# Two expert mixtures: blocks of 32 tokens on four 32-column lanes in place of blocks of 64 on two lanes

## What is computed

```python
g_sel = argmax(h @ grp_w + grp_b)                 # one of 4 groups
e_p, e_i = top_k(softmax(logits of the group's 8 experts), 2)
for each token and each of its two experts e:
    hid = silu(x @ w_gate[e]) * (x @ w_up[e])     # 1024 -> 512
    out[token] += weight * (hid @ w_down[e])      # 512 -> 1024
```

## Time and profile before

| | |
|---|---|
| median of 3 runs | 2241.99 us (2241.41 to 2243.58) |
| the profiled execution | 2241.24 us |
| its span | 2239.5 us |
| PE, weight loads, DVE, ACT busy | 95%, 62%, 49%, 27% of the span |
| read from DRAM | 614.42 MB, 281 GB/s over the span |
| of it expert weights | 64 experts of 3 slabs |
| mean granted TensorE clock | 0.991 of full speed |
| mixture 0 | from 311.6 us to 839 us |
| mixture 1 | from 1000.4 us to 1464 us |

### The profile page before, as it was taken

How to read it: one execution, slowest core, us unless ns; L and a number is a source line. 1 busy time by engine, 2 the same in 40 slices (tenths; PEclk the granted TensorE clock), 3 DMA queues, 4 the chain that set the end, 5 groups by cost and what they waited for, 6 DMA issues and landing times.

```text
span 2239.5 us, 31551 instructions
## 1 busy us (share of the span) xinstructions
PE 2134.6 (95%) x12424; PEld 1387.6 (62%) x12424; DVE 1086.9 (49%) x1971; ACT 595.2 (27%) x1200; POOL 12.7 (1%) x20
## 2 busy tenths in 40 slices
PE   7999999999898989899999999999999999999998
PEld 4744654444343437574444444478989988998997
DVE  5677541111111126642222222167888777787876
ACT  4446632211111114531111111033441012434001
POOL 0000000000000010000000000000000000000000
PEclk9999999999999999999999999999999999999999
DMA  8289268998999995248999999962345546235452
GB/s 351 76 353 427 85 254 360 380 383 346 429 381 430 428 402 221 113 157 343 427 428 428 428 429 428 426 252 107 121 170 188 188 160 254 105 118 203 185 189 97
DMA packets 50144, 629.95 MB, mean 281 GB/s; under 512 B 5888, under 2 KB 6912, under 8 KB 11904
## 3 DMA queue, kind: packets, MB, share of 16 engines
q1 hardware_dynamic: 45008, 611.30, 67.1%
q10 hardware_dynamic: 2880, 9.44, 1.0%
q0 software_dynamic: 2160, 7.87, 0.9%
HBM read 614.42 MB, written 14.16 MB: 281 GB/s over the span
## 4 chain that ended last, share of the span: by engine, by line
PE 70%; DMA 16%; DVE 9%; ACT 2%; issue 1%; SPq 0%; POOL 0%; ACTq 0%; POOLq 0%; DVEq 0%
PE ps L1954 10%; DMA ring<-in_ex_gate 9%; PE ps L1887 7%; PE ps L1401 6%; PE ps L1402 6%; PE ps L1403 6%; DMA ring<-in_ex_up 6%; PE ps L1970 4%; PE ps L2033 4%; PE ps L2034 4%; PE ps L2035 4%; PE ps L1838 3%; PE ps L1926 2%; PE ps L1748 1%; PE ps L1424 1%
## 5 line engine op out<-in xcount | busy, mean ns | idle before, releaser
L1954 PE MATMUL ps<-ring,E 128*64 128x512 f32 x1152 | 261.2, 611 | 19.6 <-DMA ring<-in_ex_up 18.2
L1403 PE MATMUL ps<-hn_hi,w_lo 128*128 128x256 f32 x928 | 262.4, 283 | 0.0
L1887 PE MATMUL ps<-ring,E 128*64 128x512 f32 x992 | 219.4, 594 | 7.9 <-DMA ring<-in_ex_gate 7.6
L1954 PEld LDWEIGHTS ps<-ring,E 128*64 128x64 f32 x1152 | 87.7, 141 | 189.7 <-issue 189.7
L2820 DVE TENSOR_TENSOR E<-E,ps 128x512 f32<-128x512 f32 x18 | 12.4, 688 | 358.2 <-PE ps L1954 358.2
L1403 PEld LDWEIGHTS ps<-hn_hi,w_lo 128*128 128x128 f32 x928 | 177.8, 192 | 0.0
L1887 PEld LDWEIGHTS ps<-ring,E 128*64 128x64 f32 x992 | 73.2, 137 | 138.8 <-issue 137.9
L1401 PE MATMUL ps<-hn_hi,w_lo 128*128 128x256 f32 x480 | 138.2, 288 | 1.6 <-DVE w_lo L2922 1.6
L1124 ACT ACTIVATE hT<-ps 128x512 f32<-128x512 f32 x70 | 41.8, 599 | 368.1 <-PE ps L1838 368.1
L1402 PE MATMUL ps<-hn_lo,w_lo 128*128 128x256 f32 x480 | 135.7, 283 | 0.0
L2922 DVE TENSOR_TENSOR w_lo<-ring,w_hi 128x4096 fp32r<-128x4096 f32 x30 | 132.8, 4426 | 1.0
(11 more groups left out here) (574 smaller groups left out, 3832.2 us busy)
## 6 DMA issues: line engine op xcount, KB each, us to landing
ring<-in_ex_up SPq DMA_DIRECT2D x64, 2048.0 KB, 15.9
ring<-in_ex_gate SPq DMA_DIRECT2D x62, 2048.0 KB, 17.0
ring<-in_ex_down SPq DMA_DIRECT2D x60, 2048.0 KB, 14.7
ring<-in_w_layer SPq DMA_DIRECT2D x56, 2048.0 KB, 8.2
ring<-in_w_static SPq DMA_DIRECT2D x33, 2048.0 KB, 15.6
y_rows<-E ACTq DMA_DIRECT2D x36, 256.0 KB, 8.4
ring<-in_ex_down SPq DMA_DIRECT2D x8, 1024.0 KB, 13.3
E<-in_w_layer SPq DMA_DIRECT2D x2, 2048.0 KB, 13.3
```

The costliest lines, as they stand in the source:

```text
L1403: return pe.matmul(out, lo, xhi, start=False, stop=last)
L1887: ins = pe.matmul(ps[half(u), 2 + w, :], xg[:, k, half(u)], weights, start=k == 0, stop=k == KC - 1)
L1954: ins = pe.matmul(ps[half(u), 2 + w, :], xg[:, k, half(u)], slab(2 * w + u, (KC, DE))[:, k, :], start=k == 0, stop=k == KC - 1)
```

## The change

`SLOTS` becomes 32 and the number of output lanes four. Lane (u, h) is rows (2u + h) * 32 to (2u + h + 1) * 32. The 32 tokens of block u stand twice in the pair's 128 rows, in lanes (u, 0) and (u, 1); for gate and up, lane h takes half h of the 512 hidden columns, for down it takes half h of the 1024 output columns. So a product of gate and up has 256 columns instead of 512, there are four of them for a chunk instead of two, and down has four products of 512 columns for a chunk as before, but each on a lane of its own. The results take half a bank or one bank in place of one or two, and the operations on them are half as wide; there are two transposes of hidden values instead of four. The gather, `turn` and `build` keep their sizes. `selT` gets two masked copies, one for each output half (`lane`, a new constant). A store of outputs is 128 KB for a lane instead of 256 KB. The plan has up to 64 blocks instead of 48. For the counts above there are 51 blocks (26 pairs) in mixture 0 and 32 blocks (16 pairs) in mixture 1. Cut to its core:

```diff
-SLOTS = 64
-PAIR = 2 * SLOTS
-MAXB = 48
+SLOTS = 32
+LANES = 2 * SLOTS
+PAIR = 2 * LANES
+MAXB = 64
...
+        def lane(u, h):
+            return slice((2 * u + h) * SLOTS, (2 * u + h + 1) * SLOTS)
...
-                    act.activation(g2B, ps[:, 6:8, :].rearrange("p a b -> p (a b)"), ACT.Copy).then_inc(mod_ready, 1)
+                    act.activation(g2B, ps[:, 6, :], ACT.Copy).then_inc(mod_ready, 1)
...
-                    act.activation(silu_g, ps[:, 2, :], ACT.Silu).then_inc(sems["sg_ready"], 1)
+                    act.activation(silu_g, ps[:, 2, 0:HALF], ACT.Silu).then_inc(sems["sg_ready"], 1)
...
-                    act.activation(yb, ps[:, 6:8, :].rearrange("p a b -> p (a b)"), ACT.Copy).then_inc(sems["y_ready"], 1)
+                    act.activation(yb, ps[:, 6, :], ACT.Copy).then_inc(sems["y_ready"], 1)
                     act.wait_ge(sems["y_ready"], i + 2)
                     for u in range(2):
-                        act.dma_start(y_rows[bass.ds(lane_block(u, pairs, i) * SLOTS, SLOTS), :], yb[u * SLOTS:(u + 1) * SLOTS, :]).then_inc(sems["y_stored"], 16)
+                        act.dma_start(y_rows[bass.ds(lane_block(u, pairs, i) * SLOTS, SLOTS), :].rearrange("s (c n) -> c s n", c=2),
+                                      yb[u * LANES:(u + 1) * LANES, :]).then_inc(sems["y_stored"], 16)
...
-                for c in range(2):
-                    act.activation(y_hi0[:, c * 512:c * 512 + 512], ps[:, 6 + c, :], ACT.Copy, scale=wsl[:, 0:1]).then_inc(yhi_ready, 1)
+                act.activation(y_hi0[:, :], ps[:, 6, :], ACT.Copy, scale=wsl[:, 0:1]).then_inc(yhi_ready, 2)
...
+                def inner(w, k, weights):
+                    for u in range(2):
+                        for h in range(2):
+                            ins = pe.matmul(ps[lane(u, h), 2 + w, 0:HALF], xg[:, k, lane(u, h)], weights[u][:, h * HALF:(h + 1) * HALF],
+                                            start=k == 0, stop=k == KC - 1)
+                    return ins
+
+                def down(m, bank):
+                    for u in range(2):
+                        for c in range(2):
+                            ins = pe.matmul(ps[lane(u, c), bank, :], hid[:, m % 2, lane(u, m // 2)], slab(4 + u, (EC, D))[:, m, half_cols(c)],
+                                            start=m == 0, stop=m == EC - 1)
+                    return ins
+
+                def turn_hid(bank):
+                    for m in range(EC // 2):
+                        ins = pe.transpose(ps[:, bank, m * P:(m + 1) * P], htmp[:, m * P:(m + 1) * P], ident)
+                    ins.then_inc(sems["hidt_mm"], 1)
...
                         for k in range(KC):
-                            for u in range(2):
-                                ins = pe.matmul(ps[half(u), 2 + w, :], xg[:, k, half(u)], slab(2 * w + u, (KC, DE))[:, k, :],
-                                                start=k == 0, stop=k == KC - 1)
+                            ins = inner(w, k, [slab(2 * w + u, (KC, DE))[:, k, :] for u in range(2)])
                         ins.then_inc(sems["gu_mm"], 1)
...
-                    dve.tensor_tensor(htmp, silu_g, ps[:, 3, :], ALU.mult).then_inc(sems["hid_ready"], 1)
+                    dve.tensor_tensor(htmp, silu_g, ps[:, 3, 0:HALF], ALU.mult).then_inc(sems["hid_ready"], 1)
...
-                    dve.tensor_copy(selT[:, :], ps[:, 0, 0:NX]).then_inc(selt_ready, 1)
+                    for c in range(2):
+                        ins = dve.tensor_scalar(selT[:, c, :], ps[:, 0, 0:NX], cc("lane")[:, c:c + 1], None, ALU.mult)
+                    ins.then_inc(selt_ready, 1)
...
-                    ins = dve.scalar_tensor_tensor(yb[:, 0:512], ps[:, 0, :], wsl[:, 0:1], g2B[:, 0:512], ALU.mult, ALU.mult)
-                    if last:
-                        ins.then_inc(yw_ready, 1)
-                    dve.scalar_tensor_tensor(yb[:, 512:D], ps[:, 1, :], wsl[:, 0:1], g2B[:, 512:D], ALU.mult, ALU.mult).then_inc(yw_ready, 1)
+                    dve.scalar_tensor_tensor(yb, ps[:, 0, :], wsl[:, 0:1], g2B, ALU.mult, ALU.mult).then_inc(yw_ready, 1)
...
-                    link(dve.tensor_scalar(halves[:, 1:2], halves[:, 0:1], float(PAIR), -float(SLOTS), ALU.mult, ALU.add))
-                    link(dve.tensor_scalar(iota2[:, SLOTS:PAIR], iota[:, 0:SLOTS], halves[:, 1:2], None, ALU.add))
+                    link(dve.tensor_scalar(halves[:, 1:2], halves[:, 0:1], float(LANES), -float(SLOTS), ALU.mult, ALU.add))
+                    for h in range(2):
+                        ins = dve.tensor_scalar(iota2[:, lane(1, h)], iota[:, 0:SLOTS], halves[:, 1:2], None, ALU.add)
+                    link(ins)
```

More of the change, by code:

```diff
@@ L191, in hybrid_program @@
         sel = rounded("sel", [P, NTM, PAIR], "E", 0)
[L193 to L196, removed]
+        y_hi = rounded("y_hi", [P, 512], "cat", 2048)
+        y_lo = rounded("y_lo", [P, 512], "cat", 3072)
+        selT = rounded("selT", [P, 2, NX], "sqb", 1024)
+        g2B = sqb[:, 0, :]
         selw = sqb[:, 3, :].rearrange("p (n k s) -> p n k s", n=QT, k=2)
@@ L236, in hybrid_program @@
         fresh = E[0:1, 2560:2560 + MAXB + 1]
-        below = E[:, 2624:2624 + MAXB // 2]
+        below = E[:, 2632:2632 + MAXB // 2]
         own = E[0:1, 2688:2688 + MAXB]
-        halves = E[:, 2656:2658]
+        halves = E[:, 2672:2674]
         iota2 = E[:, 4608:4608 + PAIR]
@@ L1884, in pair1 @@
                         for k in range(KC):
-                            for u in range(2):
-                                weights = SPARE[u][k] if spare and w == 0 else slab(2 * w + u, (KC, DE))[:, k, :]
-                                ins = pe.matmul(ps[half(u), 2 + w, :], xg[:, k, half(u)], weights,
-                                                start=k == 0, stop=k == KC - 1)
+                            ins = inner(w, k, [SPARE[u][k] if spare and w == 0 else slab(2 * w + u, (KC, DE))[:, k, :] for u in range(2)])
                         ins.then_inc(sems["gu_mm"], 1)
@@ L1923, in pair1 @@
                             pe.wait_ge(guess_in, HALVED[1])
-                        for c in range(2):
-                            for u in range(2):
-                                ins = pe.matmul(ps[half(u), c, :], hid[:, m, half(u)], slab(4 + u, (EC, D))[:, m, c * 512:(c + 1) * 512],
-                                                start=m == 0, stop=m == EC - 1)
+                        ins = down(m, 0)
                     ins.then_inc(sems["y_mm"], 1)
@@ L1958, in pair @@
                     pe.wait_ge(sems["hid_ready"], i + 1)
-                    for m in range(EC):
-                        ins = pe.transpose(ps[:, 4, m * P:(m + 1) * P], htmp[:, m * P:(m + 1) * P], ident)
-                    ins.then_inc(sems["hidt_mm"], 1)
+                    turn_hid(4)
                     turn(i + 2)
@@ L1967, in pair @@
                     for m in range(EC):
-                        for c in range(2):
-                            for u in range(2):
-                                ins = pe.matmul(ps[half(u), 6 + c, :], hid[:, m, half(u)], slab(4 + u, (EC, D))[:, m, c * 512:(c + 1) * 512],
-                                                start=m == 0, stop=m == EC - 1)
+                        ins = down(m, 6)
                     ins.then_inc(sems["y_mm"], 1)
@@ L1980, in experts @@
                     for k in range(KC):
-                        for u in range(2):
-                            ins = pe.matmul(ps[half(u), 2 + w, :], xg[:, k, half(u)], slab(2 * w + u, (KC, DE))[:, k, :], start=k == 0, stop=k == KC - 1)
+                        ins = inner(w, k, [slab(2 * w + u, (KC, DE))[:, k, :] for u in range(2)])
                     ins.then_inc(sems["gu_mm"], 1)
@@ L3235, in constants @@
     t["rank"] = p
+    t["lane"] = p // SLOTS % 2 == np.arange(2)[None, :]
     t["eps"] = np.full((P, 1), EPS)
@@ L3337 @@
     out = nc.dram_tensor("out_T", (P, QT, D), F32, kind="ExternalOutput").ap()
-    y_rows = nc.dram_tensor("y_rows", (MAXB * SLOTS + PAIR, D), F32, kind="Internal").ap()
+    y_rows = nc.dram_tensor("y_rows", (MAXB * SLOTS + LANES, D), F32, kind="Internal").ap()
     hybrid_program(nc, *args, out, y_rows)
```

99 lines of the change are left out of this document (49 added, 50 removed).

## The result

The changed kernel takes 2396.38 us (median of four runs, 2392.66 to 2399.45) against 2241.70 of the kernel before: a ratio of 1.0688, 95% interval 1.067 to 1.0707. The forecast was 2223.5 us, faster. One execution of a later kernel, the one with one lane pair on two engines, took 4800.90 us, which no record explains; it is left out of that kernel's time and ratio. Most lines of the new profile stand 6 lower in the code than the old ones, or a few more. The products of both mixtures now stand in helpers of one line each: gate and up in L1879, down in L1886, the transposes of hidden values in L1892; the gather is L1846 and the last scatter L1959.

What follows compares the result with a forecast made beforehand. Both mixtures sit close to two limits: PE's 26 to 28 us a pair and the DMA queue's 29.4 with two loads. 2241.2 - 6.8 (mixture 0) - 11.7 (mixture 1) = 2222.7, median 2223.5 us; range 2209 to 2240.

Steps and rivals of the forecast that it cites:

- At no cost: Items priced at nothing: half-width copies, second mask of `selT`, `y_rows` stores, larger plan in mixture 1 (+0.3 us).
- Lanes out of step: Slower rival, pairs of mixture 0: lanes drain between steps; at 0.09 us a step +43, 2266 us; chance 0.09.
- the clock: Slower rival: PE stays at 1.2 GHz through all of mixture 1, 2299 us; chance 0.05 together with blocks.
- an extra pair: Rival: a mixture 1 expert over 32 tokens costs a whole pair, 29.4 us; chance 0.05 together with the clock.
- Lanes: Four lanes on PE: gate and up 3.47 us each, down 3.6, a pair of mixture 0 15.6 us.
- Pairs of mixture 0: 26 pairs for 19: last down but one ends 4.8 us earlier, bounds -8 and -3; two-load pairs 27.3 us.
- The rule: Slab timing in mixture 0: 4.93 us of queue, usable 4.0 later; a wait over 2.5 us adds 1.9.
- The end of mixture 0: Chain behind the last down but one: -1.4 us for copy and last quarter of down, -0.6 for operations behind.
- Mixture 1: Transfers end 13.2 us earlier (9.8 of queue idle, 3.4 from earlier first issue), less 1.5: -11.7 us.
- The clock term: End of mixture 1: +1.5 us for the scatter at the lower clock after a longer wait.
- The sum: Profiled 2241.2 - 6.8 (mixture 0) - 11.7 (mixture 1) = 2222.7 us; expected median 2223.5 us.
- more than forecast: Faster case: slabs usable sooner, no clock term, -13 in mixture 0 and -14 in mixture 1, 2213 us; chance 0.08.

Runs made afterwards that it cites:

- one lane pair on two engines: Changed kernel, the store of lane pair 0 cut by halves of the columns, that of lane pair 1 left as it was: 2298.72 us, ratio 1.0256.
- four stores: Changed kernel, each lane pair's y_rows store cut in two by halves of the columns, 32 rows x 512 columns each: 2232.10 us, ratio 0.9953.

## Why the prediction was wrong, point by point

- **The step that failed** stands under "At no cost": "the `y_rows` stores (same engine count, half the bytes)". The bytes were halved (9.44 to 6.55 MB), the engine count went from 16 to 2. I priced the store by its bytes (0.6 us of queue for 1.2) and did not read the pattern's new outer dimension, which the diff shows. What it measured: 46.4 us from issue to landing where 8.4 had been hidden, 328.4 us of ScalarE's waits, 160 us on mixture 0. The same sentence should have named what hides the store: the next copy comes one pair later, so it was hidden up to 26.0 us and would be up to 15.6 after. The time of a pair had been the cover, and the change shortened it as well.
- **None of the rivals held it.** Lanes out of step, the clock and an extra pair were the slower ones; the range ended at 2240. A rival that made the stores land late was missing.
- **Lanes.** 3.47 us for gate or up: measured 3.64 to 3.66 with the edges, down 3.64 for 3.6, and a pair without waits 15.7 us for 15.6 (copies at 328.6, 344.3, 360.0 with four stores). Lanes out of step are excluded. The Trainium skill's speedup of 3.07 (TensorE: Matmul & The Clock Gate, Part 3) is stated for four tiles that split the array by rows (K = 32); these lanes split it by columns at K = 128, and the loss that I worked out from it doesn't appear.
- **Pairs of mixture 0.** With four stores the last copy starts at 806.51 in place of 808.92: -2.4, forecast -4.8, outside the bounds of -8 and -3. Pairs with two loads took 28.2 us on average (25.4 to 29.6), forecast 27.3. The rule charged 1.9 us for the clock behind a long wait, under a condition that no row shows; behind the waits of 2.7 to 6.7 us, gate and up took 4.94 to 6.55 us in place of 3.66 (one, behind 2.67 us, took 3.66).
- **The end of mixture 0.** Forecast 2.0 us shorter, measured 3.6 longer with four stores: from the copy to SP's next loads 34.4 us, where it was 30.9 (808.92 to 839.78). POOL starts its gathers 13.6 us behind the copy (11.8 before), since the last store packet itself ends 12.3 us behind it (10.5 before); ScalarE's weighing comes 1.3 us later still, and the transposes and the last quarter of down run at the low clock: that quarter takes 1.94 us as before, for half the work, where I had -1.0. Together that is +1.2 at SP's loads; at the first gate product (1000.76) it is +0.4, in place of -6.8. Why the stores and the gathers land later stays open.
- **Mixture 1.** The first slab of the next layer is usable 445.2 us behind the first gate product, 456.8 before: -11.6, forecast -13.2. The clock term, +1.5, was +2.4: the scatter L1961 takes 6.11 us for 3.70. PE is busy for 70 us in 100 (1300 to 1400 us) at a mean clock of 0.86, where I had near 60, and within the pairs it costs nothing, since the queue stays at 429 GB/s. The clock rival had the clock fall, but to 0.5 all through, and its price didn't come. The Trainium skill's "HAM oscillation" (TensorE: Matmul & The Clock Gate) describes such a falling clock between waits for DMA, and this trace agrees (0.86); of mixture 1's time only the last scatter's 2.4 us hang on it here.
- **The sum.** With the stores mended: +0.4 - 11.6 + 2.2 (behind the slab, the scatter in it) = -9.0 us between the profiled spans, against -18.5 forecast. The sign of the change's idea was right, its size half. One sum of the prediction is off: "more than forecast" takes -13 for mixture 0, where its own bounds give -8 - 1.4 - 0.6 = -10, and even -13 and -14 make 2215 us and not 2213.

The lines of the kernel with four stores that the last points rest on, the end of mixture 0 and of mixture 1:

```profile
806.51 0.60 ACT L1172 ACTIVATE E<-ps 128x512 f32<-128x512 f32 x1 [2.66 <-PE ps L1888]
...
820.15 1.01 POOL L3196 DMA_INDIRECT cat<-y_rows,sloti  x1 [502.78 <-POOLq L3192]
...
831.92 1.15 ACT L1188 ACTIVATE cat<-cat,wts 128x1024 f32<-128x1024 f32 x1 [15.70 <-DMA cat<-y_rows,sloti]
...
838.89 1.94 PE L1888 MATMUL ps<-ring,E 128*32 128x512 f32 x8
...
840.95 3.00 SPq L636 DMA_DIRECT2D ring<-in_w_static  x6
...
1445.98 3.90 ACT L1145 ACTIVATE w_lo<-ring 128x1024 fp32r<-128x1024 f32 x4 [17.93 <-DMA ring<-in_w_layer]
...
1449.01 6.11 PE L1961 MATMUL ps<-E,selT 128*128 128x512 f32 x8 [5.43 <-DVE E L2852]
```

## What to carry to other kernels

When a store's or a load's pattern changes, read its outermost dimension before its bytes: a rearrangement that puts a dimension of 2 outside leaves 2 engines, and the packet counts on the page show it (packets less rows, divided by the DMAs). Beside a stream of large packets such a transfer took, here, its packets per engine times the sum of both packet times (44.5 for 46.4 us, 27.7 for 29.6, 22.2 for 22.7); compare that with the time until its buffer is wanted again, and look at what stands behind that wait on the same engine. Where the pattern can't be turned, cut it into DMAs with a long outer dimension: four stores of 32 rows in place of two of 64 cost the kernel before nothing measurable.

## What the runs showed of the hardware that was not expected

- A DMA from ScalarE with 64 partitions on one side and an outer dimension of 2 on the other has 2 closing packets of 4 bytes, one with 62 rows 2 as well, 51 and 13 rows 3 and 13 (2880 packets for 36 of each: 2304 rows and 576), 32 rows 16.
- An engine with work from two queues took their packets in turn, whatever their sizes: 2 KB of y paid for 16 KB of weights each time (a turn of 0.69 us; 46.4 us for 64, by the packets 44.5; 29.6 for 36 of 4 KB, by the packets 27.7). The Trainium skill's page DMA: Bandwidth & Descriptors, section "Queues, rings and completion order", states such turns for packets of some 9 to 17 descriptors. The packets in these records are rows of 2, 4 or 16 KB; how many descriptors one holds no record tells.
- With two buffers for y, and so more stores under way on the same two engines, issuing two stores held ScalarE for 13.69 us.
- With stores on 2 engines the DMA rate was 402 GB/s in one stretch of mixture 0 and 138 in another, so the mean shows little: in the changed kernel the queue stood idle while ScalarE's wait for a landing held back everything behind it.
